# Two transformer layers' mixers on one core: the recurrence's attention in 32-row squares of the array, the 64-channel scores two at a time

## The chip, the cores and the metric

The kernel runs on one core of a Trainium2 chip. The metric is device time in microseconds (us). TensorE (PE) does the matrix products and loads its weights beside them (PEld); VectorE (DVE), ScalarE (ACT) and GpSimd (POOL) do the rest, SyncE (SP) issues the loads. The granted TensorE clock is at full speed (2.4 GHz) in practically the whole span.

## What is computed

A two-layer block with a recurrence (HGRN2) and sparse attention, followed by a second two-layer block: feed-forward, a mixture of retention, latent attention and differential attention, cross-attention, feed-forward. 256 tokens, 1024 channels, float32. The parts that the change touches:

```python
# hgrn2_mixer, 8 heads of 128 channels: q_, k_ and the summed log gate b_ of one chunk of 64
diff = jnp.where(causal[:, :, None], b_[:, :, :, None, :] - b_[:, :, None, :, :], -jnp.inf)
attn = jnp.einsum('bhtk,bhsk,bhtsk->bhts', q_, k_, jnp.exp(diff))
...
# retention, 4 heads of 64 channels
scores = jnp.einsum('bcnhd,bcmhd->bchnm', qc, kc) * intra_decay.astype(dt)
...
# diff_attention, 4 heads, two sets (j) of 64 channels
sc = jnp.einsum('bqhjd,bkhjd->bhjqk', qb, k) * scale
p = masked_softmax_2(sc, chunk_causal_mask(i, s))
w = p[:, :, 0] - lam * p[:, :, 1]
```

## The kernel before

A planner (`make_plan`) writes one list of steps; five programs, one for each engine, walk through it and pick the steps that are theirs. Each engine runs its part in that order, and semaphores carry the order between engines. `spread` and `weave` interleave streams: a main stream (recurrence, attention) yields, and at each yield a filling stream (dense projections) is advanced by a given amount of planned work (`plan.work`, in columns, 2400 to a microsecond). So the order depends on the costs that the steps of the filling stream declare.

Dense products are float32 made from rounded high and low halves: a piece of 128x2048 weights is loaded to `raw`, rounded by ACT (L2325) into `high`, its rest taken by DVE (L2541), and used by PE in the three lines L2030, L2034 and L2040. These products fill most of the time. Products of plain float32 (the recurrence, scores, transposes) run as two instructions on PE each, so the profile counts twice the products that the program writes; each of the two is one weight load and one matmul, a pair below.

The recurrence works through the 256 tokens of four heads at once (`hgrn_heads`, called for hg = 0 and 1 in each of the two layers of the first block, four times in all). The matrix of 128 x 128 for each of two token tiles t and four heads i is made of a diagonal (`same`, L2194) and of levels 64, 32, 16, 8, 4, 2, 1 (`within`, L2216): level h holds the entries between the lower and upper half of each stretch of 2h tokens. For each level, POOL and DVE form differences of the summed gates (`level_from`), ACT takes their exponential (`level_exp`, L2495), DVE multiplies (`level_mul`, L2881), PE multiplies full 128x128 squares, eight to a level, into two banks, and DVE copies the level's entries from each bank through a mask (`within_put`, L2887, 128x512):

```python
for i in range(4):
    score = pe.matmul(bank.ap[:, i * P:i * P + P], r3[:, i, t * P:t * P + P], r3[:, i, t * P:t * P + P],
                      start=True, stop=True, skip_group_check=True)
```

Level 128, between the token tiles (`across`), is apart. After level 1, `hgrn_v` (L2226, L2228) multiplies the finished matrix with the values; tile 0 waits only for the last masked copy of its own bank. In the first block each of these groups of eight stands between other PE work.

The scores of 64 channels: `diff_attention` calls `plan.scores` (PE line L2094) four times in each layer of the second block, once for each token tile t and each set j of 64 channels; set j lies in partitions 64j to 64j+63, and PE works on one set's four heads, then side work, then the other set's. The tile t=0 has 128 keys, t=1 has 256. `ret_scores` (L2273 for 256 columns, L2276 for 128) does the same for retention: its four calls in a layer take partitions 0 to 63 twice, then 64 to 127 twice, with nothing between.

`cmp_1` (L2133), which the change leaves alone, multiplies 128x32 weights into four strips of 32 output partitions in turn; its pieces are 1 MB loads that PE uses up in under a microsecond.

## Time and profile before

| | |
|---|---|
| time, three runs | 2106.7, 2109.15, 2109.32 us (median 2109.15) |
| the profiled execution | 2107.87 us, its span 2106.1 us |
| TensorE busy | 2073.8 us (98%), 11563 matmuls |
| weight loads | 1778.2 us (84%) |
| VectorE busy | 1413.4 us (67%) |
| ScalarE busy | 1050.4 us (50%) |
| moved by DMA | 357 MB, 170 GB/s on average |
| recurrence products (L2194, L2216) | 512 pairs |

The span is one execution from first to last instruction; the execution's own time is 1.8 us longer. Busy time of PE is where at least one matmul is under way; matmuls overlap, so a mean duration is longer than the distance from one start to the next. Distances are read from the timeline.

### The profile page before, as it was taken

The page shows a single profiled execution, that of the slowest core. Times are in us where ns is not written, and L with a number is a line of the kernel's source. Part 1 is how long each engine was busy: PE and PEld are TensorE (multiplying, and loading weights), DVE is VectorE, ACT ScalarE, POOL GpSimd, SP SyncE. Part 2 cuts the span into 40 slices and gives each one's busy share as a digit, 9 for nine tenths or more (in the row PEclk, how much of TensorE's full clock was granted, in tenths as well). Part 3 has the DMA queues.
Part 4 walks back from the last instruction along what each step waited for, and adds up shares of the span by engine and source line. Part 5 has one row for each costly group of instructions (what it writes and reads, how often), then busy time and mean ns, then how long its engine had stood idle before and what let it go on. Part 6 is the DMA issues. An engine that isn't in the chain of part 4 may idle for free.

```text
span 2106.1 us, 27741 instructions
## 1 busy us (share of the span) xinstructions
PE 2073.8 (98%) x11563; PEld 1778.2 (84%) x11563; DVE 1413.4 (67%) x1806; ACT 1050.4 (50%) x1520; POOL 106.2 (5%) x121
## 2 busy tenths in 40 slices
PE   8999999999999999999999999999999999999998
PEld 7979888978888888887888888888888878888887
DVE  5766877767877766666775565675766567656655
ACT  6444646356535554455445454554544554444543
POOL 0100110010100000000000000000100000000000
PEclk9999999999999999999999999999999999999999
DMA  8363335463336664454454555565654544644552
GB/s 294 110 217 121 103 118 203 131 212 114 108 114 216 218 212 154 163 160 157 167 197 157 174 189 187 181 222 189 211 165 140 168 160 165 200 160 162 188 186 95
DMA packets 193271, 357.26 MB, mean 170 GB/s; under 512 B 8381, under 2 KB 85369, under 8 KB 193146
## 3 DMA queue, kind: packets, MB, share of 16 engines
q1 hardware_dynamic: 190410, 345.53, 49.2%
q0 software_dynamic: 2736, 9.96, 1.4%
q8 instruction: 91, 1.49, 0.3%
q14 instruction: 34, 0.28, 0.0%
HBM read 354.42 MB, written 1.05 MB: 169 GB/s over the span
## 4 chain that ended last, share of the span: by engine, by line
PE 79%; DVE 3%; DMA 1%; ACT 1%; issue 0%; POOL 0%; SPq 0%; DVEq 0%; ACTq 0%
PE bank L2030 15%; PE bank L2034 15%; PE bank L2040 14%; PE bank L2072 13%; PE bank L2076 7%; PE bank L2094 2%; PE bank L2085 2%; PE bank L2054 2%; PE bank L2060 2%; PE bank L2057 2%; PE bank L2111 1%; DVE raw_r L2541 1%; PE bank L2216 1%; PE bank L2102 1%; PE bank L2299 1%; DMA raw<-in_cmp_w_v_dram 1%
## 5 line engine op out<-in xcount | busy, mean ns | idle before, releaser
L2541 DVE TENSOR_TENSOR raw_r<-raw,high 128x2048 fp32r<-128x2048 f32 x304 | 686.2, 2267 | 77.7 <-ACT high L2325 76.6
L2325 ACT ACTIVATE high<-raw 128x2048 fp32r<-128x2048 f32 x304 | 575.3, 1896 | 228.3 <-PE bank L2040 169.0
L2030 PE MATMUL bank<-high,units_r 128*128 128x512 f32 (+1 forms) x1576 | 629.7, 400 | 3.9 <-ACT high L2325 2.6
L2034 PE MATMUL bank<-high,units_r 128*128 128x512 f32 (+1 forms) x1576 | 616.3, 391 | 2.0 <-DVE units_r L2565 1.1
L2040 PE MATMUL bank<-raw_r,units_r 128*128 128x512 f32 (+1 forms) x1576 | 422.8, 389 | 0.0
L2030 PEld LDWEIGHTS bank<-high,units_r 128*128 128x128 f32 x1576 | 297.3, 189 | 65.0 <-issue 4.0
L2034 PEld LDWEIGHTS bank<-high,units_r 128*128 128x128 f32 x1576 | 297.5, 189 | 61.5 <-DVE units_r L2562 2.2
L2040 PEld LDWEIGHTS bank<-raw_r,units_r 128*128 128x128 f32 x1576 | 295.8, 188 | 62.5 <-DVE raw_r L2541 0.7
L2072 PE MATMUL bank<-units_r,high 128*128 128x512 f32 x1152 | 288.2, 392 | 0.0
L2072 PEld LDWEIGHTS bank<-units_r,high 128*128 128x128 f32 x1152 | 208.4, 189 | 38.1
L2076 PEld LDWEIGHTS bank<-units_r,raw_r 128*128 128x128 f32 x1152 | 157.2, 190 | 11.2
L2076 PE MATMUL bank<-units_r,raw_r 128*128 128x256 f32 x1152 | 160.6, 282 | 0.0
L2902 DVE TENSOR_TENSOR units<-bank,units 128x256 f32<-128x256 f32 x144 | 60.4, 422 | 147.1 <-ACT units L2358 147.1
L2358 ACT ACTIVATE units<-bank 128x256 f32<-128x256 f32 x144 | 54.2, 376 | 171.0 <-PE bank L2076 171.0
L3035 POOL TENSOR_TENSOR stat<-stat,halfs 128x1 f32<-128x1 f32 (+2 forms) x64 | 56.0, 875 | 1614.4 <-DVE stat L2650 841.2
L2390 ACT ACTIVATE units<-units,stat 128x256 f32<-128x256 f32 (+2 forms) x176 | 74.0, 422 | 121.6 <-DVE stat L2611 121.6
L2342 ACT ACTIVATE units_r<-bank 128x512 fp32r<-128x512 f32 x92 | 51.1, 599 | 141.4 <-PE bank L2085 107.1
L2054 PE MATMUL bank<-units_r,high 128*128 128x256 f32 x448 | 114.7, 288 | 0.0
L2057 PE MATMUL bank<-units_r,high 128*128 128x256 f32 x448 | 112.1, 283 | 0.0
L2565 DVE TENSOR_TENSOR units_r<-bank,units_r 128x512 fp32r<-128x512 f32 x84 | 54.2, 684 | 54.9 <-ACT units_r L2342 54.9
L2054 PEld LDWEIGHTS bank<-units_r,high 128*128 128x128 f32 x448 | 85.7, 191 | 0.3
L2057 PEld LDWEIGHTS bank<-units_r,high 128*128 128x128 f32 x448 | 85.8, 191 | 0.3
(263 smaller groups left out, 2164.9 us busy)
## 6 DMA issues: line engine op xcount, KB each, us to landing
raw<-in_ffn_w_dram SPq DMA_DIRECT2D x132, 1024.0 KB, 5.1
raw<-in_w_in_dram SPq DMA_DIRECT2D x108, 1024.0 KB, 5.2
raw<-in_w_out_dram SPq DMA_DIRECT2D x24, 1024.0 KB, 4.9
raw<-in_cross_wkv_dram SPq DMA_DIRECT2D x16, 1024.0 KB, 5.1
raw<-in_w_branch_dram SPq DMA_DIRECT2D x12, 1024.0 KB, 4.9
raw<-in_cross_wq_dram SPq DMA_DIRECT2D x8, 1024.0 KB, 5.2
raw<-in_cross_wo_dram SPq DMA_DIRECT2D x8, 1024.0 KB, 4.9
raw<-in_w_in_dram SPq DMA_DIRECT2D x4, 832.0 KB, 4.5
```

Of the source, the lines that this page charges most:

```text
L2030: pe.matmul(o, h.high(k0 + k)[:, span], p.hi[k][:, cols], start=start and k == 0, stop=False, skip_group_check=True)
L2034: pe.matmul(o, h.low(k0 + k)[:, span], p.hi[k][:, cols], start=False, stop=False, skip_group_check=True)
L2040: product = pe.matmul(o, h.high(k0 + k)[:, span], p.lo[k][:, cols], start=False, stop=stop and k == p.k - 1, skip_group_check=True)
L2054: pe.matmul(o, w, h.high(k0 + k), start=first and k == 0 and c % 2 == 0, stop=False, skip_group_check=True)
L2057: pe.matmul(o, w, h.low(k0 + k), start=False, stop=False, skip_group_check=True)
L2072: pe.matmul(bank.ap.rearrange("p (a s) -> p a s", a=2), p.hi[k][:, c * P:c * P + P], h.whole(k, m.units_r), start=k == 0, stop=False, skip ...
L2076: product = pe.matmul(bank.ap[:, 0:256], p.lo[k][:, c * P:c * P + P], h.high(k), start=False, stop=k == p.k - 1, skip_group_check=True)
L2325: done = act.activation(high, raw, ACT.Copy)
L2390: done = act.activation(p3[:, h, :], p3[:, h, :], ACT.Exp, bias=mx[:, h:h + 1], scale=1.0, accum_out=sm[:, h:h + 1])
L2541: done = dve.tensor_tensor(low, raw, high.bitcast(F32), ALU.subtract)
L2902: dve.tensor_tensor(dst, bank.ap[:, 0:256], dst, ALU.add).then_inc(*mark(s.vout, ("folded", name, c)))
L3035: pool.tensor_tensor(ss, ss, m.halfs[:, 0:ss.shape[1]], ALU.pow).then_inc(*mark(s.pstat, ("rstd", name)))
```

## The change

The diagonal and the levels 16 to 1 have entries only in the 32x32 squares on the diagonal. The change computes only these: 32 products of 32x32 for a level, each in the strip of 32 output partitions of its place (`blocks_of_32`), all in one bank, 256 columns of it. Their masked copies go to `near`, 128x256 (one DVE copy to a level in place of two of twice the width), and at the end four copies (two on ACT, two on DVE) put `near` in its four strips of the matrix. Level 64 becomes eight products of 64x64, level 32 sixteen of 32x32 in the strips 0 and 64 (`level_halves`); they are copied straight to their place, once on ACT for level 64, once each on ACT and DVE for level 32. The rest of the matrix is cleared by one DVE memset. `hgrn_v` waits for all of these copies, for both tiles. The table of constants is smaller by 704 columns.

For the scores of 64 channels, the products of the two sets alternate: `scores_of_two` and `ret_two` take two banks, one for each half of the partitions, and issue a product of the one half and a product of the other in turn. Of the four PE groups of `diff_attention` in a layer two are left.

```diff
@@ -54,8 +54,10 @@
     p = np.arange(P)[:, None]
     j = np.arange(P)[None, :]
     put("ident", p == j)
-    for h in (1, 2, 4, 8, 16, 32, 64):
-        put(f"m{h}", (p // (2 * h) == j // (2 * h)) & (p % (2 * h) < h) & (j % (2 * h) >= h))
+    put("ident32", (p % 32 == j)[:, 0:32])
+    q = p % 32
+    for h in (1, 2, 4, 8, 16):
+        put(f"m{h}", ((q // (2 * h) == j // (2 * h)) & (q % (2 * h) < h) & (j % (2 * h) >= h))[:, 0:32])
...
+    def scores_pair(self, names, need, nh, L, ofs, bias, scale):
...
+        per = 512 // max(L, 128)
+        units = [self.U.take() for _ in names]
+        p3s = [u.ap[:, 0:nh * L].rearrange("p (h l) -> p h l", h=nh) for u in units]
+        for q in range(0, nh, per):
+            n = min(per, nh - q)
+            banks = [self.B.take() for _ in names]
+            self.work += n * L * 4
+            self.do("scores_of_two", names=names, need=need, q=q, n=n, L=L, ofs=ofs, banks=banks)
+            for name, bank, u, p3 in zip(names, banks, units, p3s):
+                self.do("scores", name=name, q=q, n=n, L=L, bank=bank, u=u, p3=p3, bias=bias, scale=scale, of=None)
+                self.B.give(bank, ("scored", name, q))
+        return [self.soft(name, u, p3, nh, q, True) for name, u, p3 in zip(names, units, p3s)]
@@ -1235,12 +1256,15 @@
...
-            for t in range(2):
-                b = B.take()
-                plan.work += 4 * 512
-                do("same", name=H, t=t, need=[qx, kx], k_=kk, q_=q_, bank=b, dst=AT[t], after=aa.after)
-                B.give(b, ("attn", H, 0, t))
-            U.give(kk, ("pairs", H, 0, 1))
+            blocks = h3(aa.ap, 8)
+            near = a01.ap[:, 512:768]
+            b = B.take()
+            plan.work += 8 * 170
+            do("same", name=H, need=[qx, kx], k_=kk, q_=q_, bank=b, dst=near, after=a01.after)
+            B.give(b, ("attn", H, 0))
+            U.give(kk, ("pairs", H, 0))
+            do("clear", name=H, dst=blocks[:, :, 0:96], after=aa.after)
+            cleared = (*aa.after, ("cleared", H))
@@ -1275,22 +1299,30 @@
...
-                    bs = [B.take(), B.take()]
-                    for t in range(2):
-                        plan.work += 4 * 512
-                        do("within", name=H, lev=lev, t=t, R=R[li], bank=bs[t])
-                    U.give(R[li], ("pairs", H, lev, 1))
+                    b = B.take()
+                    plan.work += 8 * (256 if lev == 64 else 170)
+                    do("halves" if lev > 16 else "within", name=H, lev=lev, R=R[li], bank=b)
+                    U.give(R[li], ("pairs", H, lev))
                 yield
                 if li < 7:
                     level_mul(li + 1)
                 if li < 6:
                     level_from(li + 2)
-                if lev != 128:
-                    for t in range(2):
-                        do("within_put", name=H, lev=lev, old=old, t=t, bank=bs[t], dst=AT[t])
-                        B.give(bs[t], ("attn", H, lev, t))
+                if lev in (64, 32):
+                    for o in range(0, P, 2 * lev):
+                        made.append(plan.copy(f"{H}.a{lev}.{o}", [("pairs", H, lev)],
+                                              blocks[o:o + lev, :, o + lev:o + 2 * lev],
+                                              h3(b.ap[o:o + lev, 0:8 * lev], 8), "dve" if o else "act", cleared))
+                    B.give(b, *made[-(64 // lev):])
+                elif lev < 32:
+                    do("within_put", name=H, lev=lev, old=old, bank=b, dst=near)
+                    B.give(b, ("attn", H, lev))
                     old = lev
                 yield
+            for i in range(4):
+                strip = slice(32 * i, 32 * i + 32)
+                made.append(plan.copy(f"{H}.a{i}", [("attn", H, 1)], blocks[strip, :, strip], h3(near[strip, :], 8),
+                                      "dve" if i % 2 else "act", cleared))
             U.give(q_, ("level_q", H, 1))
             U.give(sp, ("from_k", H, 1))
             U.give(bb, ("from_k", H, 1), ("from_q", H, 1))
...
-                   need=[vt[t], *(vt[0:1] if t else ()), ("attn", H, 1, t), *([a01x] if t else [])])
+                   need=[vt[t], *(vt[0:1] if t else ()), *made, *([a01x] if t else [])])
@@ -1635,15 +1667,14 @@
...
-                    got.append(plan.scores(f"{N}.ds{t}{jj}", t_made, 4, L, of, 1, cst("chunk")[:, 256 - L:256],
...
+                                       cst("chunk")[:, 256 - L:256], 64.0 ** -0.5)
+                yield 8
                 (u1, p1, s1, soft1), (u2, p2, s2, soft2) = got
@@ -1690,12 +1721,13 @@
...
+                RS = [f"{N}.rs{i}{int(whole)}" for i in range(2)]
+                bs = [B.take(), B.take()]
+                plan.work += 2 * (256 if whole else P) * 4
+                do("ret_two", names=RS, need=t_made, r3=r3, whole=whole, banks=bs)
+                for i, (R, b) in enumerate(zip(RS, bs)):
+                    do("ret_scores", name=R, i=i, whole=whole, bank=b, dst=s0 if whole else s1)
                     B.give(b, ("decayed", R))
                     s_made.append(("decayed", R))
             U.give(rT, ("ret_scores", R))
@@ -2085,7 +2117,19 @@
...
-    def scores(name, need, q, n, L, of, steps, bank, **_):
+    def scores_of_two(names, need, q, n, L, ofs, banks, **_):
+        for e in (*need, *banks[0].after, *banks[1].after):
+            hold.wait_ge(*at(e))
+        for i in range(n):
+            for jj, bank in enumerate(banks):
+                left, right = ofs(jj, q + i)
+                score = pe.matmul(bank.ap[:, i * L:i * L + L], left, right, start=True, stop=True,
+                                  skip_group_check=True)
+        score.then_inc(*mark(s.attn, *[("scores", name, q) for name in names]))
@@ -2187,13 +2231,22 @@
...
-    def same(name, t, need, k_, q_, bank, **_):
+    def blocks_of_32(bank, left, right):
+
+
+        for t in range(2):
+            for i in range(4):
+                o = (4 * t + i) * 32
+                for strip in range(0, P, 32):
+                    span = slice(t * P + strip, t * P + strip + 32)
+                    score = pe.matmul(bank.ap[strip:strip + 32, o:o + 32], h3(left.ap, 4)[:, i, span],
+                                      h3(right.ap, 4)[:, i, span], start=True, stop=True, skip_group_check=True)
+        return score
+
+    def same(name, need, k_, q_, bank, **_):
         for n in (*need, *bank.after):
@@ -2206,16 +2259,27 @@
...
-    def within(name, lev, t, R, bank, **_):
...
             hold.wait_ge(*at(n))
         r3 = h3(R.ap, 4)
-        for i in range(4):
-            score = pe.matmul(bank.ap[:, i * P:i * P + P], r3[:, i, t * P:t * P + P], r3[:, i, t * P:t * P + P],
-                              start=True, stop=True, skip_group_check=True)
-        score.then_inc(*mark(s.attn, ("pairs", name, lev, t)))
+        for t in range(2):
+            for i in range(4):
+                o = (4 * t + i) * lev
+                for k in range(0, P, 2 * lev):
+                    score = pe.matmul(bank.ap[k:k + lev, o:o + lev], r3[:, i, t * P + k:t * P + k + lev],
+                                      r3[:, i, t * P + k + lev:t * P + k + 2 * lev], start=True, stop=True,
+                                      skip_group_check=True)
+        score.then_inc(*mark(s.attn, ("pairs", name, lev)))
+
+    def within(name, lev, R, bank, **_):
+        hold.wait_ge(*at(("level", name, lev)))
+        hold.wait_ge(*at(("level_q", name, lev)))
+        for n in bank.after:
+            hold.wait_ge(*at(n))
+        blocks_of_32(bank, R, R).then_inc(*mark(s.attn, ("pairs", name, lev)))
 
     def hgrn_v(name, t, AT, a01, vh, bank, need, **_):
         for n in (*need, *bank.after):
@@ -2264,18 +2328,19 @@
...
-            if whole:
-                score = pe.matmul(bank.ap[:, q * 256:q * 256 + 256], r3[half, 2 + q, 0:P], r3[half, q, :], start=True,
-                                  stop=True, skip_group_check=True)
-            else:
-                score = pe.matmul(bank.ap[:, q * P:q * P + P], r3[half, 2 + q, P:256], r3[half, q, P:256], start=True,
-                                  stop=True, skip_group_check=True)
-        score.then_inc(*mark(s.attn, ("ret_scores", name)))
+            for i, bank in enumerate(banks):
+                half = slice(64 * i, 64 * i + 64)
+                if whole:
+                    score = pe.matmul(bank.ap[:, q * 256:q * 256 + 256], r3[half, 2 + q, 0:P], r3[half, q, :], start=True,
+                                      stop=True, skip_group_check=True)
+                else:
+                    score = pe.matmul(bank.ap[:, q * P:q * P + P], r3[half, 2 + q, P:256], r3[half, q, P:256], start=True,
+                                      stop=True, skip_group_check=True)
+        score.then_inc(*mark(s.attn, *[("ret_scores", name) for name in names]))
 
@@ -2846,12 +2911,12 @@
...
-        dve.tensor_tensor(h3(dst, 4), h3(bank.ap, 4), bh(ident, 4), ALU.mult).then_inc(
-            *mark(s.vout, ("attn", name, 0, t)))
+        dve.tensor_tensor(h3(dst, 8), h3(bank.ap[:, 0:256], 8), bh(m.cst("ident32"), 8), ALU.mult).then_inc(
+            *mark(s.vout, ("attn", name, 0)))
@@ -2881,11 +2946,16 @@
...
+    def clear(name, dst, after, **_):
+        for n in after:
+            hold.wait_ge(*at(n))
+        dve.memset(dst, 0.0).then_inc(*mark(s.vout, ("cleared", name)))
+
+    def within_put(name, lev, old, bank, dst, **_):
+        hold.wait_ge(*at(("pairs", name, lev)))
+        hold.wait_ge(*at(("attn", name, old)))
+        dve.copy_predicated(h3(dst, 8), bh(m.cst(f"m{lev}").bitcast(I32), 8), h3(bank.ap[:, 0:256], 8)).then_inc(
+            *mark(s.vout, ("attn", name, lev)))
```

The order of the dense work around the recurrence stays the same; on each engine a group takes the place of a group. Three places in the rows of both programs (the lines below the changed functions have moved: L2040 is L2072 in the changed kernel, L2030 and L2034 are L2062 and L2066, L2085 is L2117, L2228 and L2226 are L2292 and L2290, L2576 is L2641, L2390 is L2455, L2405 is L2470).

PE, first layer, second set of heads (hg = 1), levels 64 and 32, before:

```order
L2040 MATMUL bank<-raw_r,units_r 128x512 x4
L2216 MATMUL bank<-units 128x128 x8
...
L2040 MATMUL bank<-raw_r,units_r 128x512 x4
L2216 MATMUL bank<-units 128x128 x8
L2085 MATMUL bank<-consts,units 128x128 x8
```

The same place in the changed kernel:

```order
L2072 MATMUL bank<-raw_r,units_r 128x512 x4
L2272 MATMUL bank<-units 64x64 x8
...
L2072 MATMUL bank<-raw_r,units_r 128x512 x4
L2272 MATMUL bank<-units 32x32 x16
L2117 MATMUL bank<-consts,units 128x128 x8
```

The groups stand where they stood, with eight dense products (left out) between them; L2272 is `level_halves`.

PE at the end of the same set: level 1 and the product with the values (`hgrn_v`), before and then changed:

```order
L2040 MATMUL bank<-raw_r,units_r 128x512 x4
L2216 MATMUL bank<-units 128x128 x8
L2228 MATMUL bank<-units 128x128 x4
L2226 MATMUL bank<-units 128x128
```

```order
L2072 MATMUL bank<-raw_r,units_r 128x512 x4
L2242 MATMUL bank<-units 32x32 x32
L2292 MATMUL bank<-units 128x128 x4
L2290 MATMUL bank<-units 128x128
```

Nothing stands between the level (L2242 is in `blocks_of_32`) and the product that needs the finished matrix.

DVE at the end of the first set of heads (hg = 0), first layer, before and then changed, and ACT there in the changed kernel:

```order
L2611 TENSOR_SCALAR stat<-stat 128x4
L2887 COPY_PREDICATED units<-consts,bank 128x512 x2
L2576 SCALAR_TENSOR_TENSOR units<-units,bank 128x512 x2
L2790 RECIPROCAL stat<-stat 128x4
```

```order
L2676 TENSOR_SCALAR stat<-stat 128x4
L2957 COPY_PREDICATED units<-consts,bank 128x256
L2641 SCALAR_TENSOR_TENSOR units<-units,bank 128x512 x2
L2637 COPY units<-units 32x8x32 x2
L2855 RECIPROCAL stat<-stat 128x4
```

```order
L2455 ACTIVATE units,stat<-units,stat 128x128 x4
L2417 ACTIVATE units<-units 32x8x32 x2
L2470 ACTIVATE units<-bank 128x512
```

The last copies into the strips come behind two DVE operations of another stream (L2641) and four ACT operations of another (L2455); L2470 reads the result of `hgrn_v`.

## Rows read from the trace of the kernel before

**Rows 1.** The page: busy time of each engine, share of the span, instructions.

```profile
PE 2073.8 (98%) x11563; PEld 1778.2 (84%) x11563; DVE 1413.4 (67%) x1806; ACT 1050.4 (50%) x1520; POOL 106.2 (5%) x121
```

**Rows 2.** Groups of weight loads by form: shapes, count; busy us, mean ns; idle before.

```profile
L2216 PEld LDWEIGHTS bank<-units 128*128 128x128 f32 x448 | 53.5, 191 | 5.6 <-issue 4.2
...
L2133 PEld LDWEIGHTS bank<-raw,units 128*32 128x32 f32 x256 | 6.6, 110 | 4.3 <-DMA raw<-in_cmp_w_v_dram 3.5 <-issue 0.7
```

**Rows 3.** Timeline of PE at 82 us: start, length; engine, line, what, count.

```profile
82.30 1.07 PE L2040 MATMUL bank<-raw_r,units_r 128*128 128x512 f32 x4
83.21 1.95 PE L2216 MATMUL bank<-units 128*128 128x128 f32 x16
...
85.22 0.40 PE L2034 MATMUL bank<-high,units_r 128*128 128x512 f32 x1
```

**Rows 4.** Timeline of PE from 92 us.

```profile
92.26 1.07 PE L2040 MATMUL bank<-raw_r,units_r 128*128 128x512 f32 x4
93.26 1.95 PE L2133 MATMUL bank<-raw,units 128*32 128x128 f32 x64
95.14 2.05 PE L2216 MATMUL bank<-units 128*128 128x128 f32 x16
...
97.27 0.39 PE L2034 MATMUL bank<-high,units_r 128*128 128x512 f32 x1
```

**Rows 5.** Line L2133 in the stretch 93.25 to 93.28 us: count, ns min/median/max.

```profile
L2133 PEld LDWEIGHTS bank<-raw,units x4: 106/106/106, 93.3 to 93.3; 128*32 128x32 f32 x4
L2133 PE MATMUL bank<-raw,units x4: 297/297/297, 93.3 to 93.3; 128*32 128x128 f32 x4
```

**Rows 6.** Line L2143, two matmuls of 32 columns: timeline, then all of the line.

```profile
125.63 0.30 PE L2143 MATMUL bank<-consts,units 128*128 128x32 f32 x2
```

```profile
L2143 PE MATMUL bank<-consts,units x8: 190/232/273, 99.8 to 436.8; 128*128 128x32 f32 x8
```

**Rows 7.** Timeline of PE: two score groups of differential attention, first layer.

```profile
963.44 1.99 PE L2094 MATMUL bank<-units 64*128 64x256 f32 x8
...
965.70 0.40 PE L2034 MATMUL bank<-high,units_r 128*128 128x512 f32 x1
...
971.07 1.16 PE L2094 MATMUL bank<-units 64*128 64x128 f32 x8
...
972.49 0.39 PE L2034 MATMUL bank<-high,units_r 128*128 128x512 f32 x1
```

**Rows 8.** Timeline of PE: scores of retention, first layer.

```profile
877.12 1.13 PE L2273 MATMUL bank<-units 64*128 64x256 f32 x4
878.09 0.27 PE L2276 MATMUL bank<-units 64*128 64x128 f32 x1
878.10 0.48 PE L2273 MATMUL bank<-units 64*128 64x256 f32 x1
...
879.60 0.44 PE L2102 MATMUL bank<-consts,units 128*128 128x128 f32 x2
```

**Rows 9.** Groups by form: a DVE operation of 128x256.

```profile
L2902 DVE TENSOR_TENSOR units<-bank,units 128x256 f32<-128x256 f32 x144 | 60.4, 422 | 147.1 <-ACT units L2358 147.1
```

**Rows 10.** Timelines of DVE and PE at the end of the first heads.

```profile
171.80 1.36 DVE L2887 COPY_PREDICATED units<-consts,bank 128x512 f32<-128x512 int32 x2
173.05 1.27 DVE L2576 SCALAR_TENSOR_TENSOR units<-units,bank 128x512 f32<-128x512 f32 x2
...
172.82 1.05 PE L2228 MATMUL bank<-units 128*128 128x128 f32 x8
```

**Rows 11.** Timelines of PE and DVE at the end of the second heads.

```profile
290.43 1.03 PE L2085 MATMUL bank<-consts,units 128*128 128x128 f32 x8
...
295.95 2.02 PE L2216 MATMUL bank<-units 128*128 128x128 f32 x16
...
291.69 1.29 DVE L2565 TENSOR_TENSOR units_r<-bank,units_r 128x512 fp32r<-128x512 f32 x2 [2.34 <-ACT units_r L2342]
```

**Rows 12.** Timeline of PE: a wait for a load.

```profile
115.62 1.08 PE L2133 MATMUL bank<-raw,units 128*32 128x128 f32 x32 [1.23 <-DMA raw<-in_cmp_w_v_dram]
```

51 lines of the change are left out of this document (20 added, 31 removed).

## The prediction

> **What bounds the kernel now.** I read the page first: PE is busy for 98% of the span, DVE for 67%, ACT for 50% [rows 1]. So what the change takes from PE comes off the end, unless another engine or a load then ends last; and every short wait of PE is to be sought in the timeline, since only some 32 us of idle are there. The timeline of PE then gives the price of each kind of group, always as the distance between two starts, since matmuls overlap. A dense product of 512 columns follows the one before after 0.227 us: four of them span 1.07 us, the last alone lasts 0.39, and (1.07 - 0.39) / 3 = 0.227 [rows 3].
>
> **The groups of the recurrence.** The change touches 32 groups of eight products, that is 16 pairs of weight load and matmul each: in each of four calls the diagonal and seven levels. What one costs: from the start of the four L2040 to the start of L2034 behind the next L2030 are 85.22 - 82.30 = 2.92 us [rows 3]; less five dense products (1.13) leaves **1.79 us**, 0.112 for a pair.
>
> What a group in strips costs is read from L2133, which has 32-column weights in four strips of output partitions too, with 128 moving columns. From 92.26 to 97.27 are 5.01 us [rows 4]; less 1.13 and less the L2216 group that lies between (1.79) leaves 2.09 us for 64 pairs. Four matmuls and four loads start within 0.03 us of each other [rows 5], so the strips work side by side and a round of four pairs is the unit. From first to last start are 1.95 - 0.27 = 1.68 us for fifteen rounds and a bit, 0.109 each; sixteen rounds are 1.75. What is left, **0.34 us**, is the price of entering and leaving: as I read it, PE runs empty before it, the first load is not hidden, and the same again behind it.
>
> How long a round is with 32 moving columns, no row shows. Lower bound: two matmuls of 32 columns (with full weights) start 0.30 - 0.273 = 0.027 us apart, once their weights are there [rows 6]. The load: one of 128 columns takes 0.191 us, one of 32 takes 0.110 [rows 2], 0.081 less, and loads of 128 columns keep up with a pair each 0.112; so 0.112 - 0.081 = 0.031. Upper bound: 0.109, as with 128 moving columns. I take 0.031, since both rows that have one of the two operands short lie near it. A group of 32 products is 64 pairs, 16 rounds: 16 x 0.031 + 0.34 = 0.84 us, 0.95 less than before. Level 32 has 32 pairs in two strips, 16 rounds again: also 0.95 less. Level 64 has 16 pairs one after the other; between 0.031 and 0.112 a weight load of 64 columns is at 0.058: 16 x 0.058 + 0.34 = 1.27, 0.52 less.
>
> - 24 groups (diagonal, levels 16 to 1, four calls): 22.8 us
> - level 32: 4 x 0.95 = 3.8; level 64: 4 x 0.52 = 2.1
> - twice level 32 stands next to L2133, which is in strips already, and one entry and leaving goes: 0.7
>
> **The scores.** A group of one half with 256 columns costs 965.70 - 963.44 - 0.227 = 2.03 us from its start and about 0.09 before it (93.26 against 92.26 + 4 x 0.227), 2.12 in all; with 128 columns 972.49 - 971.07 - 0.227 + 0.09 = 1.28 [rows 4, 7]. Where retention passes from one half to the other, a matmul of each half starts within 0.01 us of the other [rows 8]: the halves work side by side. So two groups merged into one, in turns, take the time of one: 3.40 us in each of two layers, 6.8. Lower bound: nothing, if they take turns instead. Retention takes 879.60 - 877.12 = 2.48 us; with 256 columns a pair takes 0.216 (2.03 less some 0.3, by eight), so four rounds of 0.216, four of 0.112 and 0.2 to leave make 1.51: 0.97 less, 1.9 for both layers. Together 8.7.
>
> **What is given back.** Each of these stands twice, once a layer.
> (a) First set of heads: `hgrn_v` starts at 172.82, after two masked copies at 171.80 [rows 10]. Now one masked copy of 0.42 [rows 9], the two silu products that stood behind it (1.27), and two strip copies of some 0.35 each (a 128x256 operation less its overlap) come first: 171.80 + 0.42 + 1.27 + 0.70 + 0.1 for the signal = 174.3. PE waits 1.5 us.
> (b) Second set: `hgrn_v` follows level 1 at once. Drain and signal (0.1), masked copy (0.4), two strip copies on each engine (0.7) and a signal (0.1) lie open: 1.2 us.
> (c) Its level 1 starts at 295.95 when DVE is ready, at the end of a chain from L2085 at 290.43 over ACT to DVE (L2565, with 2.34 us of waiting for ACT) [rows 11]. The level-2 group lies between on PE; its 0.95 turn into a wait, less 0.1 that I allow for slack: 0.85.
> (d) L2133 at 115.62 already waits 1.23 us for its load [rows 12], issued some 12 us before; one level group lies in that stretch and ends earlier for nothing: 0.95.
> Sum 4.5, twice 9.0 us.
>
> DVE gains more than it gets: a masked copy of 256 columns for two of 512 at every level, so 0.9 us a group, as much as PE, and the pace of the two stays together in the long stretches. The memset of 768 columns and the ACT copies lie beside dense products, with DVE and ACT idle for a third and half of the time [rows 1]; without that cover they would cost some 3 us a call. The smaller table of constants is loaded while PE works on earlier pieces: nothing. The side work of the scores is yielded in one lump of the same size: nothing. The loads in general follow PE's pace, with less time for the same bytes (1.5%).
>
> **Sum.** 22.8 + 3.8 + 2.1 + 0.7 + 8.7 = 38.1 us gained, 9.0 given back: 29 us. Against the profiled execution of 2107.9 us this is **2079 us**; the median of the runs is 1.3 us above that execution, well inside the margin. A measurement of this kernel tells 0.2% (4 us) from no change.
>
> The Trainium skill speaks against the change on the page TensorEngine Tiling (Array Packing), section Performance Considerations: a matmul has about 60 cycles of overhead, so one with a single column lasts as long as one with 60, and the tiling factor should not be taken from a dimension that is small already. By it, as an estimate, a pass of 32 columns would count as 60 at 2.4 GHz, 25 ns, and two passes 50 ns in place of my 31; 16 x 19 ns in 28 groups make the time 2087.5. The rows on L2143, two starts 27 ns apart, do not bear it out.
>
> **The rivals.**
> 1. *In a short round load and matmul of a strip do not overlap.* Then a round is 0.031 + 0.027 = 0.058 us; 28 groups lose 16 x 0.027 = 0.43 each, 12 us: **2091**. For it: no row has both operands short. Against: at L2133 both fit into 0.109, and loads of 128 columns hide behind matmuls [rows 2, 3]. Chance 0.10. The skill's rule above ends between this and my forecast.
> 2. *The recurrence waits for DVE.* If four more level groups in each layer meet a multiply that is not done, they lose their 0.95: 7.6 us, **2086.5**. For it: (c) shows that DVE's multiply can come last. Against: DVE's own saving. Chance 0.10.
> 3. *The halves take turns.* Then scores gain only the transitions: some 8 us less, **2087**. Against: rows 8. Chance 0.04.
> 4. *The strips do not load side by side; slower than before.* If the loads of short groups pass one at a time, a pair costs 0.031 and a group 64 x 0.031 + 0.34 = 2.32, 0.53 more than before: 24 x 0.53 = 12.7 lost; level 32 gains 0.46 x 4 = 1.8, level 64 2.1, L2133 0.7, scores 5.9 (with both halves' loads in line too, those of 128 columns save only their transitions); (a) and (b) stay, 5.4. Net 7.6 us slower: **2115.5**. It decides from about 0.026 us a pair on. For it: 64 loads in 1.7 us at L2133 are 0.027 each. Against: four loads within 0.03 us, each 0.106 long [rows 5]. Chance 0.05.
> 5. *One start each 0.027 us on the whole engine*, the mean at L2133 and the distance at L2143. Then a group is 64 x 0.027 + 0.34 = 2.07, 0.28 more: 6.7 lost, level 32 gains 2.4, and with 2.1, 0.7, 8.7 gained and 5.4 lost the time is **2106**. Against: four starts within 0.03 us [rows 5]. Chance 0.03. The Trainium skill states such a floor on TensorE: Matmul & The Clock Gate (Part 1): start to start never below about 25 ns however few the columns; by its figure, as an estimate, 2103.
>
> **How the numbers follow.** My forecast has 0.68; its own range is 2072 to 2086: a round of 29 to 36 ns (2 us), the entry at 0.30 to 0.40 (2 us), the give-backs at 6 to 13 us. Rivals 1 to 3 lie at 2086 to 2091, so **2068 to 2093** leaves out rivals 4 and 5 (0.08) and the tails. Faster by over 0.2%: the forecast, rivals 1 to 3, 0.92; within 0.2%: rival 5, 0.03; slower: rival 4, 0.05.
>
> **What would show it.** In the profile of the changed kernel: the L2242 group of 64 pairs spans about 0.5 us plus one matmul's length (0.19), four starts within some 20 ns; from L2072 to L2066 behind it are 1.97 us in place of 2.92. Level 64 takes 1.27 us. The merged scores take 2.1 and 1.3 us. PE waits about 1.5 us before L2292 in the first set and 1.2 in the second, for the strip copies; some 0.9 before the last level of the second; 2.2 for the cmp_w_v load. DVE's busy time falls by some 25 us. The forecast is wrong if the group spans over 1 us, or if new waits of PE come to more than 15 us together.

## The result and the profile after

| | before | after |
|---|---|---|
| median of the runs, us | 2107.93 (2106.49 to 2109.32) | 2096.68 (2095.56 to 2097.16) |
| profiled execution: time / span, us | 2107.87 / 2106.1 | 2097.16 / 2095.4 |
| mean granted clock | 0.999 | 0.992 |

The ratio is 0.9942, 95% interval 0.9928 to 0.9956: the change makes the kernel 11.2 us faster. I had forecast 29 us and 2079, with 2068 to 2093 as the range; the direction was right, the size was not, and the time lies outside the range. 18 us are missing. The medians leave out a fourth run of the changed kernel, which took 4177 us at a granted clock of 1.000 and of which there is no trace.

The page of the changed kernel, busy time by engine, answers to [rows 1]. DVE has lost 26 us, as forecast (25), PE 27.6, and PE is still at 98%:

```profile
PE 2046.2 (98%) x12779; PEld 1745.4 (83%) x12779; DVE 1387.3 (66%) x1782; ACT 1055.2 (50%) x1536; POOL 106.8 (5%) x121
```

**The groups came out as forecast.** The timeline of PE (start, length, engine, line, what, count), in the places of [rows 3, 4, 7, 8]; L2242 are the squares of 32, L2272 levels 64 and 32, L2177 the strips that were there before, L2126 the merged scores, L2338 and L2341 retention:

```profile
151.09 1.07 PE L2072 MATMUL bank<-raw_r,units_r 128*128 128x512 f32 x4
152.09 0.76 PE L2242 MATMUL bank<-units 128*32 128x32 f32 x64
152.78 0.50 PE L2062 MATMUL bank<-high,units_r 128*128 128x512 f32 x1
153.12 0.40 PE L2066 MATMUL bank<-high,units_r 128*128 128x512 f32 x1
...
92.08 1.95 PE L2177 MATMUL bank<-raw,units 128*32 128x128 f32 x64
93.85 0.68 PE L2272 MATMUL bank<-units 128*32 128x32 f32 x32
94.46 0.50 PE L2062 MATMUL bank<-high,units_r 128*128 128x512 f32 x1
...
964.92 2.00 PE L2126 MATMUL bank<-units 64*128 64x256 f32 x16
966.84 0.50 PE L2062 MATMUL bank<-high,units_r 128*128 128x512 f32 x1
...
874.04 1.13 PE L2338 MATMUL bank<-units 64*128 64x256 f32 x8
875.00 0.61 PE L2341 MATMUL bank<-units 64*128 64x128 f32 x8
875.54 0.50 PE L2062 MATMUL bank<-high,units_r 128*128 128x512 f32 x1
```

From L2072 to the L2066 behind the group are 153.12 - 151.09 = 2.03 us where 2.92 stood before and I had expected 1.97: the group costs 0.90 where I had 0.84. Sixteen matmuls of both halves with 256 columns span 2.00 us, where eight of one half spanned 1.99 before [rows 7]: the halves do work side by side. Retention takes 875.54 - 874.04 = 1.50 us (forecast 1.51). Level 32 behind the strips starts the next product after 0.61 us.

So the gain was made, and then given back. To see where, I lined up the dense products of the two traces (L2040 before with L2072 after; there are 1656 of each, in the same order) and noted at each the lead of the changed kernel. It grows by 0.85 to 0.95 us at each strip group. In each layer of the second block it grows by 4.4 us in all: 0.98 are retention's (2.48 to 1.50 us) and 3.4 those of the two merged pairs of scores (the single steps of the lead there, such as +2.17, -0.87, +2.17 and +1.36, are no prices, because a merged group and some of the side work stand at other places in the order than in before). In the first block it falls back at the same few places in both layers: by 3.8 and 4.7 us around the `cmp_w_v` loads, 1.2 and 1.2 at the first keys behind them, 1.8 and 1.8 ahead of the first `hgrn_v`, 2.9 and 2.9 at the end of the second heads.

**Two things stand at these places.** First, waits of PE. The groups of waits after (what waited, for what; us in total, times, longest):

```profile
PE bank L2146 <- DVE units L2860: 7.4, 5, 2.3
PE bank L2177 <- DMA raw<-in_cmp_w_v_dram: 7.0, 4, 3.2
PE bank L2292 <- ACT units L2417: 6.4, 4, 1.6
PE bank L2242 <- DVE units L2946: 4.3, 4, 2.0
```

and those of before at the same places (there was no wait ahead of `hgrn_v`):

```profile
PE bank L2102 <- DVE units L2795: 4.4, 2, 2.3
PE bank L2133 <- DMA raw<-in_cmp_w_v_dram: 3.0, 2, 1.8
...
PE bank L2216 <- DVE units L2881: 2.1, 2, 1.6
```

That is 3.0 + 4.0 + 6.4 + 2.2 = 15.6 us of new waits, for which my sum had 9.0.

Second, the clock. Behind such waits TensorE's granted clock stands at its lower level, 1.2 GHz (0.50 in the rows). The stretches of 4 us after; the columns are length, busy time with instructions of PE, PEld, DVE, ACT, POOL, then the granted clock, the DMA share and GB/s:

```profile
112.00:116.00 4.00, 1.84 (x34) 1.46 (x34) 0.25 (x1) 0.00 (x0) 0.21 (x1) 0.83 0.80 274
116.00:120.00 4.00, 4.00 (x14) 3.49 (x14) 0.65 (x4) 1.91 (x1) 0.83 (x1) 0.50 0.02 9
120.00:124.00 4.00, 4.00 (x20) 3.31 (x19) 0.84 (x4) 0.00 (x0) 0.00 (x0) 0.82 0.16 23
...
296.00:300.00 4.00, 4.00 (x23) 3.92 (x22) 0.85 (x2) 0.96 (x2) 1.01 (x1) 0.63 0.06 20
424.00:428.00 4.00, 3.25 (x41) 2.86 (x41) 0.29 (x1) 0.48 (x1) 1.04 (x1) 0.65 0.49 177
428.00:432.00 4.00, 4.00 (x11) 3.13 (x11) 0.61 (x3) 1.43 (x1) 0.00 (x0) 0.50 0.00 0
...
524.00:528.00 4.00, 4.00 (x21) 4.00 (x22) 3.96 (x5) 3.22 (x11) 0.00 (x0) 0.57 0.48 199
```

and the only two of before below 0.97, the end left out:

```profile
116.00:120.00 4.00, 4.00 (x42) 3.32 (x31) 0.90 (x4) 0.67 (x1) 1.04 (x1) 0.70 0.38 137
120.00:124.00 4.00, 4.00 (x20) 3.34 (x20) 0.96 (x4) 1.24 (x1) 0.00 (x0) 0.87 0.19 22
```

In the changed kernel's stretch 116 to 120 PE does 14 matmuls where a full clock allows 17 or 18, and the dense products there start 0.43 us apart in place of 0.227. What it costs can be estimated from the rows: a stretch of 4 us at a granted clock c does the work of 4c us, so it loses 4 (1 - c). Over all stretches of the span below 0.97, the last few us left out, this makes **13.6 us after** (twelve stretches) **and 1.7 us before** (two, at 116 to 124). The Trainium skill has the same formula (TensorE: Matmul & The Clock Gate, Part 1: cold time times one less the ratio of the clocks) and tells there of a kernel whose waits for loads make the clock swing. This trace agrees in that the lower clock stands behind the loads at 116 and 424 us; it stands behind waits for DVE and ACT as well.

My theory 1 was therefore: of the missing 18 us, some 12 are the lower clock that follows PE's waits (a low stretch of the clock is called a spell below), and 6 to 7 are waits that I had priced too low or not at all. The rival: the waits are all, and the clock is incidental, since PE would only wait longer at the next place.

### The profile page after: what moved, and what is told of

It is laid out like the page before. It is cut to its first block, busy times and chain, and to the rows that moved or that the text cites. A ratio compares the mean times of both kernels' runs of the same rounds, so it can differ in the third digit from the quotient of the medians.

```text
span 2095.4 us, 30152 instructions
## 1 busy us (share of the span) xinstructions
PE 2046.2 (98%) x12779; PEld 1745.4 (83%) x12779; DVE 1387.3 (66%) x1782; ACT 1055.2 (50%) x1536; POOL 106.8 (5%) x121
## 3 DMA queue, kind: packets, MB, share of 16 engines
HBM read 354.06 MB, written 1.05 MB: 169 GB/s over the span
## 4 chain that ended last, share of the span: by engine, by line
PE 78%; DVE 3%; ACT 1%; DMA 1%; issue 0%; POOL 0%; SPq 0%; DVEq 0%; ACTq 0%
PE bank L2062 15%; PE bank L2066 15%; PE bank L2072 14%; PE bank L2104 13%; PE bank L2108 7%; PE bank L2117 2%; PE bank L2138 2%; PE bank L2086 2%; PE bank L2089 2%; PE bank L2092 2%; PE bank L2155 1%; DVE raw_r L2606 1%; PE bank L2146 1%; PE bank L2364 1%; DMA raw<-in_cmp_w_v_dram 1%; PE bank L2312 0%
## 5 line engine op out<-in xcount | busy, mean ns | idle before, releaser
L2390 ACT ACTIVATE high<-raw 128x2048 fp32r<-128x2048 f32 x304 | 575.0, 1896 | 225.7 <-PE bank L2072 171.4
L2062 PE MATMUL bank<-high,units_r 128*128 128x512 f32 (+1 forms) x1576 | 631.7, 401 | 3.7 <-ACT high L2390 2.3
L2066 PE MATMUL bank<-high,units_r 128*128 128x512 f32 (+1 forms) x1576 | 617.8, 392 | 2.0 <-DVE units_r L2630 1.1
L2072 PE MATMUL bank<-raw_r,units_r 128*128 128x512 f32 (+1 forms) x1576 | 423.5, 389 | 0.0
L2062 PEld LDWEIGHTS bank<-high,units_r 128*128 128x128 f32 x1576 | 298.2, 189 | 65.3 <-issue 3.3
L2066 PEld LDWEIGHTS bank<-high,units_r 128*128 128x128 f32 x1576 | 298.4, 189 | 62.0 <-DVE units_r L2627 2.2
L2072 PEld LDWEIGHTS bank<-raw_r,units_r 128*128 128x128 f32 x1576 | 296.5, 188 | 62.9 <-DVE raw_r L2606 0.7
L2104 PEld LDWEIGHTS bank<-units_r,high 128*128 128x128 f32 x1152 | 208.4, 189 | 38.1
L2455 ACT ACTIVATE units<-units,stat 128x256 f32<-128x256 f32 (+2 forms) x176 | 73.9, 421 | 116.4 <-DVE stat L2676 116.4
```

The lines of the kernel that those rows point to most:

```text
L2062: pe.matmul(o, h.high(k0 + k)[:, span], p.hi[k][:, cols], start=start and k == 0, stop=False, skip_group_check=True)
L2066: pe.matmul(o, h.low(k0 + k)[:, span], p.hi[k][:, cols], start=False, stop=False, skip_group_check=True)
L2072: product = pe.matmul(o, h.high(k0 + k)[:, span], p.lo[k][:, cols], start=False, stop=stop and k == p.k - 1, skip_group_check=True)
L2104: pe.matmul(bank.ap.rearrange("p (a s) -> p a s", a=2), p.hi[k][:, c * P:c * P + P], h.whole(k, m.units_r), start=k == 0, stop=False, skip ...
L2390: done = act.activation(high, raw, ACT.Copy)
L2455: done = act.activation(p3[:, h, :], p3[:, h, :], ACT.Exp, bias=mx[:, h:h + 1], scale=1.0, accum_out=sm[:, h:h + 1])
```

## The experiments

Each kernel was timed against before on the same chip. Where I take a difference to the changed kernel, it is to its 2096.7 us; a second measurement of it stands below (2095.4), so differences are good to about 1.5 us.

**1 and 2: the two halves of the change alone.** `e1_scores` is before with `scores_pair`, `scores_of_two` and `ret_two`; `e2_recurrence` is before with the squares of 32, level 32 and 64 in parts, the memset and the strip copies.

```diff
 e1_scores
+    def scores_of_two(names, need, q, n, L, ofs, banks, **_):
...
+    def ret_two(names, need, r3, whole, banks, **_):
 e2_recurrence
+    def blocks_of_32(bank, left, right):
...
+    def level_halves(name, lev, R, bank, **_):
...
+    def clear(name, dst, after, **_):
```

> The kernel before with the scores of two halves merged and nothing else of the change. The ledger of dense products in the two traces gives each merged pair +2.14 us and retention +1.36: 8.7 us as predicted, so 2099.3 us (ratio 0.9959) and the granted clock as before (one spell below 0.9 in the middle, at 116 to 124 us). If the loss of the full change sits with the scores (halves that take turns, a side job that comes too late), the time stays above 2104.

> The kernel before with the recurrence's part of the change alone. The prediction's terms give 20 us less (28.7 of groups less 9 given back), 2087.5. Theory 1 (PE's new waits in the recurrence stretches cost about 6 us more than I priced, and behind them TensorE's granted clock stands at 1.2 GHz for 27 us in all, which costs another 12) expects 2105.5 (what is left of the 11.2 us when the scores' 8.7 are taken off) and the six spells at about 116, 143, 297, 428, 526 and 608 us. The rival (the two parts disturb each other in the middle, where both change the order) expects 2092 or less and no such spells.

`e1_scores`: 2098.6 us, ratio 0.9953 (0.9936 to 0.9970), 9.3 us less; no stretch of its trace is below full clock but the end. The scores' terms give 8.7 of this. Up to 877 us its PE does what it does in before, with a wait of 1.05 us for the same load (1.23 in before), and the spell of before is not there: its 1.7 us count for the scores by chance. `e2_recurrence`: 2103.4 us, ratio 0.9976 (0.9967 to 0.9986), with these stretches among others:

```profile
116.00:120.00 4.00, 4.00 (x13) 3.42 (x13) 0.61 (x3) 1.91 (x1) 0.47 (x1) 0.50 0.02 7
...
424.00:428.00 4.00, 4.00 (x39) 3.37 (x31) 0.90 (x4) 1.84 (x1) 1.04 (x1) 0.50 0.09 30
428.00:432.00 4.00, 4.00 (x11) 3.13 (x10) 0.00 (x0) 0.07 (x1) 0.00 (x0) 0.50 0.00 0
```

All the low clock comes with the recurrence's part (11.9 us by the formula), none with the scores. The rival of two parts that disturb each other falls: 2.1 us off the 2105.5 that theory 1 gave, 16 off the 2087.5 of my terms. Of the spells expected, those at 297 and 608 us are not in this trace, which is, with `e1_scores`, the first sign that a spell is not tied to one wait.

**3 and 5: PE's idle time filled.** The decisive pair. The waits stay, but PE multiplies the identity with itself while it waits; the result is overwritten, or stands in columns that nobody reads.

```diff
+    def fill(bank, count, cols=slice(0, 128), start=True):
+        if count:
+            for n in bank.after:
+                hold.wait_ge(*at(n))
+        for i in range(count):
+            pe.matmul(bank.ap[:, cols], ident, ident, start=start, stop=start, ...)
+
     def hgrn_v(name, t, AT, a01, vh, bank, need, **_):
+        if t == 0:
+            fill(bank, 6)
```

> The changed kernel with idle time of PE filled: products of the identity with itself into a free bank (or its unused columns) ahead of nine of the waits, just under as many as fit into each wait (0.112 us each): 8, 20 and 26 ahead of the waits for the cmp_w_v load, 9 and 18 ahead of keys, 15 and 4 ahead of level 4 and 7 ahead of level 1, 13 ahead of the first hgrn_v. They take no wait away and what they write is overwritten or not read. Theory 1 (the half clock that follows the waits is what is missing): granted clock back at 0.99 or more in the windows behind the waits, 10 to 13 us less than the changed kernel, 2085. Rival (the waits and what they wait for are the whole loss, the clock comes with them and changes nothing since PE waits again anyway): no change, or 1 to 2 us slower by the fillers that overrun, 2097 to 2099.

> e3_fill with half as many fillers (4, 10 and 13 ahead of the loads, 4, 4 and 9 ahead of keys, 8 and 2 ahead of level 4, 3 ahead of level 1, 6 ahead of hgrn_v). In e3_fill each product of the identity ran as two matmuls, 0.22 us, so that the fillers were twice as long as the waits: the clock came back to 0.998 and the time rose all the same, by what overran. Now they end just inside the waits. Theory 1 (half clock behind the waits costs about 12 us): clock 0.997 or more, 2085 to 2088. Rival (the clock costs nothing): 2096 to 2098.

`e3_fill` was a miss of mine, but a useful one: 2102.7 us, 6 us slower than the changed kernel although its clock was back at 0.998. Its fillers were twice too long (ahead of the first `hgrn_v` 13 products are 26 matmuls in the trace and span 3.06 us, for a wait of 1.60), and PE was late by the rest. By itself it speaks for neither theory.

`e5_fill_half` decides: **2086.1 us**, ratio 0.9896 (0.9883 to 0.9910), 10.6 us less than the changed kernel, with the waits filled and none taken away. PE in its trace at the second load of the first layer and ahead of the first `hgrn_v`:

```profile
112.49 2.50 PE L2242 MATMUL bank<-consts 128*128 128x128 f32 x20
115.01 1.08 PE L2180 MATMUL bank<-raw,units 128*32 128x128 f32 x32
...
167.80 1.50 PE L2242 MATMUL bank<-consts 128*128 128x128 f32 x12
169.59 1.13 PE L2305 MATMUL bank<-units 128*128 128x128 f32 x8 [0.30 <-ACT units L2430]
```

and its stretches where the changed kernel had 0.83, 0.50, 0.82 and 0.63:

```profile
112.00:116.00 4.00, 3.97 (x74) 3.41 (x64) 0.62 (x2) 0.00 (x0) 0.00 (x0) 1.00 1.02 332
116.00:120.00 4.00, 4.00 (x27) 3.45 (x23) 0.90 (x4) 1.40 (x1) 1.04 (x1) 1.00 0.06 22
120.00:124.00 4.00, 4.00 (x23) 3.43 (x23) 2.34 (x7) 0.52 (x1) 0.00 (x0) 1.00 0.68 222
296.00:300.00 4.00, 3.84 (x20) 2.90 (x19) 3.71 (x7) 1.23 (x2) 2.63 (x4) 1.00 0.05 11
```

Work that is of no use made the kernel 10.6 us faster. Its lead over the changed kernel, dense product by dense product, grows where the spells were, by 3.2 us at 116, 1.9 at 142, 1.6 at 297, 3.5 at 425, 1.6 at 526 and 1.7 at 608 us. The rival, by which nothing should change, is out. One spell was new, at 208 to 216 us, behind a wait of 2.12 us that both kernels have and that I had not filled; there the lead falls by 1.3.

**4: another order of the levels.** Squares first and the across-chunk level last, so that the strip copies have three groups to hide behind.

```diff
-            levels = (128, 64, 32, 16, 8, 4, 2, 1)
+            levels = (16, 8, 4, 2, 1, 64, 32, 128)
...
+                if lev == 1:
+                    for i in range(4):
+                        strip = slice(32 * i, 32 * i + 32)
+                        made.append(plan.copy(f"{H}.a{i}", [("attn", H, 1)], blocks[strip, :, strip], ...
                 yield
-            for i in range(4):
-                strip = slice(32 * i, 32 * i + 32)
...
```

> The changed kernel with its levels in the order 16, 8, 4, 2, 1, 64, 32, 128 and the four strip copies behind level 1, so that three groups lie between them and hgrn_v. The wait of 1.6 us ahead of hgrn_v (four times, 6.4 us) should shrink to 0.3 or less each: 5.2 us less by the waits alone, 2091.5. Theory 1 adds the half clock behind the second set's end (two spells of 3.4 us, 1.7 us each): 2088. If the time stays over 2095, the wait has moved to another place (level 128's multiply, which now comes last on DVE).

2091.7 us, ratio 0.9919 (0.9905 to 0.9934), 5.0 us less. The wait for the strip copies is gone from the trace; what remains at the end of the second heads is 0.90 us ahead of level 128. Here is PE at the end of the first heads, where `hgrn_v` (L2293) now follows without a wait, and at that of the second:

```profile
173.95 1.05 PE L2293 MATMUL bank<-units 128*128 128x128 f32 x8
...
294.22 1.13 PE L2259 MATMUL bank<-units 128*128 128x128 f32 x8 [0.90 <-issue]
295.19 1.06 PE L2293 MATMUL bank<-units 128*128 128x128 f32 x8
```

The low stretches at 296 and 604 are gone, but others have come (216 to 220, 452 to 456): by the formula it loses 15.3 us, where the changed kernel loses 13.6. With the clock's cost off both it is 6.7 us shorter, about the 6.4 of the waits that are gone; 1.7 of that go to the clock again. That the time came out at the 2091.5 of the waits alone is luck in part, and theory 1's figure of 2088 was too low, because it tied each spell to its wait.

**6: the memset on POOL.** `clear` moved from DVE's program to POOL's, nothing else.

```diff
-        dve.memset(dst, 0.0).then_inc(*mark(s.vout, ("cleared", name)))
+        pool.memset(dst, 0.0).then_inc(*mark(s.pstep, ("cleared", name)))
```

> The changed kernel with the memset of 128x768 on POOL in place of DVE. If the memset (0.70 us in a busy stretch of DVE) is what makes PE wait 0.67 us for L2860 at 240 us and the like in the second layer, 1.2 us less: 2095.5. If it lies beside other work, as I had priced it: no difference (2096.7).

2094.8 us, ratio 0.9942 (0.9929 to 0.9956), the changed kernel's own ratio: not told apart from no difference. The wait of 0.67 us at 240 us is absent from its trace; the rest of the 1.9 us between the medians is within what the clock's low stretches vary by (12.0 us by the formula, 13.6 in the changed kernel).

**7 and 8: what a round costs, and what the strips do.** `e7_double` makes each round of four products twice, `e8_serial` takes all products of a strip before the next strip.

```diff
 e8_serial
-        for t in range(2):
-            for i in range(4):
-                o = (4 * t + i) * 32
-                for strip in range(0, P, 32):
+        for strip in range(0, P, 32):
+            for t in range(2):
+                for i in range(4):
+                    o = (4 * t + i) * 32
```

> The changed kernel with each round of four products of the 24 strip groups made twice (the same values into the same place): 16 rounds more in each group. By my split of a group into 16 x 0.031 for the rounds and 0.34 for entering and leaving: 24 x 0.50 = 12 us more, 2108.5. If the entry is the small part and a round takes 0.05: 24 x 0.8 = 19, 2116. If a part of it lies in waits that are there anyway, less than 10.

> The changed kernel with the products of a strip group in another order: all eight of one strip, then the next strip, so that the one behind it is in the same strip. If four strips side by side are what makes a round cheap, a pair in one strip takes 0.031 (load) to 0.058 (load and columns one after the other): 64 pairs are 2.0 to 3.7 us and a group 1.5 to 3 us longer; 24 groups 36 to 72 us more, 2133 to 2169. If the array takes a start every 0.01 us in any order, no difference.

`e8_serial`: 2111.9 us, ratio 1.0013 (1.0001 to 1.0024). The same group as above, with the same 64 pairs:

```profile
151.26 1.91 PE L2242 MATMUL bank<-units 128*32 128x32 f32 x64
153.10 0.50 PE L2062 MATMUL bank<-high,units_r 128*128 128x512 f32 x1
```

1.84 us to the next start in place of 0.69, 1.15 more. The mean distance from start to start is (1.91 - 0.196) / 63 = 27 ns here, over four strips in turn (0.76 - 0.196) / 63 = 9 ns (0.196 is one matmul's length in this group). The single starts say more: inside a strip they lie 31 to 32 ns apart, the 0.031 of the prediction, and the mean is lower because the last few of a strip and the first few of the next run side by side (starts 5 to 6 and 26 to 27 ns apart by turns). Over four strips in turn a round of four takes 32 to 34 ns, as long as one pair takes alone. Strip after strip, the whole gain of the squares is gone: the group costs 0.90 + 1.15 = 2.05 us, more than the 1.79 of before and what rival 5 gave it (2.07). 24 groups make 27.6 us; the time rose by 15.2, below my range of 36 to 72 (its lower end had every pair at 31 ns and a group 1.5 us longer; the mean is 27 and a group 1.15). Of the rest 6.8 us are waits that shrank, as PE arrives later (loads 7.0 to 5.0, keys 7.4 to 4.4, L2946 4.3 to 2.5), and 5.3 the low clock (8.3 us by the formula in place of 13.6).

`e7_double`: 2117.1 us, ratio 1.0044 (1.0028 to 1.0061), 20.5 us more where I expected 12. The lead falls by 0.50 to 0.55 us at a plain group, so a round of four is 0.031 to 0.034. Sixteen of them off the 0.90 of a group leave 0.35 to 0.40 us for entering and leaving, where I had 0.34: the split holds. The rest is something else: the program has 3072 instructions more, and twelve packets more come in through the queue for instructions (113 against 101). While the data loads still take all DMA engines (their share is 1.06 at 145 to 146 us, 0.12 at 147 to 148), PE stands still with nothing that the profile shows to wait for:

```profile
143.58 1.05 PE L2155 MATMUL bank<-short_keys,units 15*128 15x128 f32 x6
...
148.57 0.79 PE L2155 MATMUL bank<-short_keys,units 15*128 15x128 f32 x2 [3.94 <-issue]
```

Six of the eight matmuls of one group, then 3.94 us, then the other two, and a low clock behind it. Its five largest stops of this kind are 3.9, 2.2, 1.4, 1.3 and 0.8 us, 9.6 in all; the changed kernel has none of over 0.3. That the missing code is what PE waits for I read from this picture; I did not test it.

**9 to 12: together, and the controls.** `e9_together` joins the order of 4, the memset of 6 and fillers fitted to the waits that 4 shows. `e10_before_fill` puts fillers ahead of before's four longest waits. `e11_changed_again` is the changed kernel as it is. `e12_fill_loads` has the fillers at the `cmp_w_v` loads alone.

```diff
 e12_fill_loads (in the others the same call, at more places)
     def cmp_1(name, p, half, e4, bank, **_):
+        fill(bank, {("a0.cmp1", 0): 4, ("a0.cmp1", 1): 10, ("a1.cmp1", 1): 13}.get((name, half), 0),
+             slice(256, 384), not half)
```

> The order of e4_order, the memset on POOL as in e6_clear, and fillers as in e5_fill_half, fitted to the waits that e4_order shows (10 and 14 ahead of the loads, 4 ahead of the first keys and the products behind them, 8 and 9 ahead of the keys that wait 2.1 and 2.3 us, 5 and 1 ahead of level 64, 3 ahead of level 128 in the second set). The windows of e4_order below full clock sum to 15 us of lost time (4 us x (1 - granted clock) each, end left out). Theory 1: clock 0.998 or more and 2091.7 - 15 = 2077, a little less with the memset gone, 2075 to 2080. If the clock falls all the same at places without a filler, or fillers overrun: 2082 to 2087.

> The kernel before with fillers ahead of its four longest waits of PE (5 and 7 ahead of the cmp_w_v loads, 8 and 9 ahead of the keys that wait 2.1 and 2.3 us). The control for e5_fill_half: before had one spell of half clock of 3.4 us. Theory 1: it gets back what that spell costs, 0 to 2 us: 2106 to 2108. If fillers gain by something else than the spells, it gains as the changed kernel does, 8 us or more.

> The changed kernel as it is, again, beside e9_together and e10_before_fill on the same chip, to see whether its spells of half clock stand at the same places in a second profile. Theory 1 expects them behind the same waits (116, 143, 297, 428, 526, 608 us) and 2096.7 (ratio 0.994); if a spell is missing, its 1.7 or 3.4 us should be missing from the lead over the first profile at that place.

> The changed kernel with fillers at the cmp_w_v loads alone (4 and 10 in the first layer, 13 in the second). The two spells behind these loads are the only ones that both profiles of the changed kernel have at the same place; e5_fill_half led the changed kernel by 2.6 and 3.2 us there. Theory 1 with each spell tied to its own wait: 5.8 us less than the changed kernel, about 2090 to 2091, the other spells as they were. If a spell that is prevented only comes at a later wait instead, the gain is 2 us or less, 2093 to 2095.

`e9_together`: **2075.7 us**, ratio 0.9850 (0.9837 to 0.9864), 31.5 us less than before on the same chip, mean clock 1.000, and no low stretch but the end. It is the fastest of all. `e10_before_fill`: 2106.0, ratio 0.9990 (0.9982 to 0.9999): before gets back what its one low spell cost and no more (1.2 us of 1.7), so fillers gain nothing by themselves. `e12_fill_loads`: 2089.3, ratio 0.9910 (0.9896 to 0.9925), 7.4 less than the changed kernel for three places filled. By the lead it gained 3.1 us at each layer's loads, 6.2 where I expected 5.8. The other spells were not as they were, against the expectation: those at 142, 297 and 526 us are absent, there are new ones at 210 and 443, and all that it has cost 6.8 us, as much as the changed kernel's four that are not behind the loads.

`e11_changed_again`: 2095.4, ratio 0.9944 (0.9931 to 0.9956). The same program, and its low stretches are partly elsewhere:

```profile
116.00:120.00 4.00, 4.00 (x35) 3.38 (x24) 0.90 (x4) 1.91 (x1) 1.04 (x1) 0.50 0.05 16
...
140.00:144.00 4.00, 2.87 (x81) 2.74 (x82) 4.00 (x5) 4.00 (x5) 2.03 (x1) 1.00 1.06 388
...
216.00:220.00 4.00, 4.00 (x24) 4.00 (x23) 4.00 (x5) 4.00 (x12) 0.00 (x0) 0.63 0.31 126
296.00:300.00 4.00, 4.00 (x31) 3.75 (x31) 1.50 (x3) 1.20 (x2) 1.01 (x1) 1.00 0.27 101
424.00:428.00 4.00, 4.00 (x41) 3.49 (x42) 0.53 (x3) 1.27 (x1) 1.04 (x1) 0.50 0.28 102
```

The two behind the loads (116, 424) and the one behind the keys (528) are there again; those at 143, 297 and 608 are not, and there are new ones at 216 and 452. Where a spell is gone, the second trace gains 1.6 to 2.0 us on the first; where one is new, it loses 1.3 to 1.6. A wait of one to two us may be followed by the lower clock or not; the sum hardly changes (13.5 against 13.6).

**All kernels in one table.** The clock's cost is the sum of 4 (1 - c) over the stretches below 0.97 of the profiled execution, the end left out; the time is the median of the runs:

| kernel | time, us | clock's cost | time less it |
|---|---|---|---|
| before | 2107.9 | 1.7 | 2106.2 |
| changed | 2096.7 | 13.6 | 2083.1 |
| changed again | 2095.4 | 13.5 | 2081.9 |
| e6_clear | 2094.8 | 12.0 | 2082.8 |
| e12_fill_loads | 2089.3 | 6.8 | 2082.5 |
| e5_fill_half | 2086.1 | 1.7 | 2084.4 |
| e3_fill (fillers too long) | 2102.7 | 1.7 | 2101.0 |
| e7_double | 2117.1 | 13.6 | 2103.5 |
| e8_serial | 2111.9 | 8.3 | 2103.6 |
| e10_before_fill | 2106.0 | 0 | 2106.0 |
| e1_scores | 2098.6 | 0 | 2098.6 |
| e2_recurrence | 2103.4 | 11.9 | 2091.5 |
| e4_order | 2091.7 | 15.3 | 2076.4 |
| e9_together | 2075.7 | 0 | 2075.7 |

Five measurements of kernels that do the same useful work in the same order, at 2086 to 2097 us (the changed kernel twice, `e6_clear`, `e12_fill_loads`, `e5_fill_half`), fall within 2.5 us of each other once the clock's cost is off; so do the two with the new order, and before with its control. The runs of before agree without any trace: those with a mean granted clock of 1.000 took 2105.6 to 2107.1 us, those with 0.998 took 2108.2 to 2110.3 and those with 0.996 took 2111.7 to 2114.0. The table also says what the change is worth without the clock: 2106.2 - 2083 = 23 us, 7.6 by the scores and 14.7 by the recurrence.

## Why the prediction was wrong

**The terms of the gain were right.** Strip groups gained 0.85 to 0.95 us each (forecast 0.95). Merged scores gained 3.4 a layer and retention 0.98 (forecast 3.4 and 0.97), 8.7 in all; `e1_scores` gave 9.3, or 7.6 with the clock's cost off both. (What is expected of `e1_scores` has +2.14 for each of four pairs and +1.36 for each of two retentions; these are steps of the lead and do not add up to its 8.7.) What was gained and given back adds up as well: 11.2 measured, 15.6 of waits and 11.9 of clock make 38.7, where the sum had 38.1. That strips and halves work side by side, the point against rivals 1, 3, 4 and 5, holds: 9 ns from start to start over four strips. Rival 4's 31 ns a pair is what one strip alone does (`e8_serial`), and that kernel, with rival 5's 27 on the mean, shows about what the time would be if either were so, 2112. The Trainium skill's floor of about 25 ns from start to start (TensorE: Matmul & The Clock Gate, Part 1) fits the pairs within one strip, 31 to 32 ns, and not those over four, 9 on the mean. Its 60 cycles for a small matmul (TensorEngine Tiling (Array Packing), Performance Considerations), 50 ns a round by my estimate, is not borne out: 31 to 34.

**The step that failed first: the clock, put at nothing.** The list "what is given back" has the waits (a) to (d) and no word on what follows a wait, and no reason for leaving it out. Before has one low spell behind its wait of 1.23 us [rows 12]; it was in the trace, and I read over it, since 0.999 on average looks like nothing. I then forecast new waits of 0.85 to 1.5 us at eight places and costed each at its own length. The waits as they came brought 11.9 us more of lost clock, and `e5_fill_half` gave 10.6 of them back.

**The step that failed second: the sizes in the list.** New waits were 15.6 us where it had 9.0.
- (a) 1.60 each, forecast 1.5; (b) 1.57 to 1.60, forecast 1.2: right, 1.0 us short in all. Two strip copies on ACT take 0.83 to 0.85 us; I had 0.70 for a pair of about 0.35 each.
- (c) 0.90 each, forecast 0.85: right.
- (d) 0.95 a layer; it was 4.0 us for both, 2.1 more. The load comes through at its own pace, and PE gains the strip groups ahead of it as well as the one that I counted; in the first layer the other half's load was late too (1.10 us).
- Not on the list: the keys. L2146 waits for DVE 3.0 us more, 1.18 in each layer right behind the loads and 0.67 at 240 us, where the memset stood in DVE's queue (gone in `e6_clear`). "DVE gains more than it gets" is true over the span (26 us less) and not at the place where PE has just caught up with a late load.
- Level 4 of the first heads: 0.4 more.

6.6 us of waits and 11.9 of clock are 18.5, less the 0.6 by which the gains came out higher: 17.9, where 17.7 were missing (2096.7 less 2079).

**The rivals.** None was it. Rival 2, waits for DVE's multiply, had the right kind but 7.6 us; L2946 costs 2.2 more. My condition of failure, "new waits of more than 15 us", was met at 15.6. The time lies 3.7 us above my range, because all its bounds were widths of known terms, none for a term left out.

## What to carry to other kernels

When a change shortens work on an engine that is busy 98% of the time, list the waits that it will open and price what comes behind them too: here each us of new wait cost another 0.8 us of lower clock. Look at the granted clock by stretches, not at the mean: 0.992 hid 12 us. Where the wait can't be taken away, short useless products that end just inside it bring the clock back (10.6 us here); too long, they cost more than they bring, so count what one takes in the trace first. Better is to put the last consumer of a chain behind work that doesn't need it: the order of the levels alone took 5 us off, and with the memset on POOL and fillers as well the kernel ends at 2075.7. What the clock adds has to be measured over several runs, since the same program had its spells at different places.
